# Layers: the index weights' rows scaled and signalled first, the values' up product behind a query product, the low part of y made right behind the row minima

## The chip, the cores and the metric

The kernel runs on one core of one Trainium2 chip. The metric is the device time of one execution in microseconds (us). Besides it stands the span: the time from the first to the last instruction in one profiled execution.

## The reference, cut to what matters

Two blocks follow each other on x (512 tokens, 1024 features). The first has two layers with three attention branches and a short convolution; it is the only part that the change touches.

```python
def first_block(x, ...):
    for l in range(DEPTH):                       # DEPTH = 2
        h = _rmsnorm(x, norm_g[l])
        p = _split(h @ w_in[l])
        o_a = _mla(p["a_cq"], p["a_ckv"], p["a_krope"], ...)
        o_b = _diff_attn(p["b_q"], p["b_k"], p["b_v"], ...)
        o_c = _dsa(p["c_q"], p["c_k"], p["c_v"], p["c_qidx"], p["c_kidx"], p["c_widx"], rel_bias, topk)
        o_d = _short_conv(p["d_b"], p["d_c"], p["d_h"], conv_w[l])
        y = jnp.concatenate([o_a * silu(a_gate), o_b * silu(b_gate), o_c * silu(c_gate), o_d * silu(d_gate)], -1)
        x = x + y @ w_out[l]
    return _rmsnorm(x, final_g)

# in _mla: q = rmsnorm(cq) @ w_uq;  kv = rmsnorm(ckv) @ w_ukv  -> k_nope, v
# in _dsa: score = relu(qidx . kidx);  index = sum over heads of widx * score;  top_k(index)
```

The second block (feed-forward, a mixture of dilated and block attention, cross attention, feed-forward) follows and is left as it is.

## The kernel before, in words

All matrices are kept transposed: features on the 128 partitions, the 512 tokens along a row. A product of fp32 accuracy is made of three passes over rounded parts: high times high, high times low and low times high. The weights come through a ring of four slots; ScalarE (ACT) makes the high part `whi` of a slot (L1632, one pass over 128x1024), VectorE (DVE, L2068) or GpSimd (POOL, L732) the low part `wlo`. TensorE (PE) runs the products of one column block of `w_in` as a "job" of eight chunks, three matmuls each (`products`, L963), into one of two PSUM banks `proj`; DVE or ACT evicts the bank and signals `job_free`.

Every engine has its own hand-written order; they meet through semaphores. Three places of a layer matter here.

**The index weights.** The job KR gives in one bank the index keys, the eight index weights (rows 0 to 8) and the rope part of the keys. DVE evicts it with four multiplications: `kidxT`, then `wT` (the weights, L2124), then two of `krope`, the last of which frees the bank. Between the first and the second stands `low_idx(1)`, a subtraction over 128x512 that makes a low part of the index queries (L2177); behind the last, `low_idx(2)` does that for the index keys. PE turns `wT` to token rows with four small matmuls (`turn_w`, L1041) in the middle of the job CQ0, and waits before them until the bank of KR is free (`wait_out(pe, L, "KR")`). ACT copies the result to `widx`.

**The attention steps.** A layer has 34 steps s. In a step PE makes the scores of step s (L1187), the products with the values of step s-3 (L1237), turns the probabilities of step s-2 (L1213), and then runs the fillers of that step: jobs, chunks and small products in the order of the tuple FILLERS, distributed over the steps by `fill_plan`. DVE makes `row_scales(s-1)`, `row_mins(s)` (L2112), early evictions, a piece of the top-k search, and the other evictions of the step; ACT copies the turned probabilities (L1823), makes the exponentials (L1658), and then handles the names of `ENDED[s]` one after the other: for each its copy and then, by `prepare_after`, the `whi` of the slot that hangs on this name. Names among the fillers: UKn, UVn and UQn are the up products of the MLA keys, values and queries. UK and UV all use one bank, `opsum[1]`; each waits until ACT has copied the one before (`up_out`). In step 4 PE runs UK1 and UQ1, in step 5 UV0 (L1123) and UQ2 (L1104), in step 6 UV1 and UQ3. The `whi` of the slot of GT1 hangs on UQ2. PE takes the scores of step s when the minima of step s-1 are made (`min_ready`).

**The low parts of y.** y is split chunk by chunk for the output product: ACT makes `yhi` at step `Y_HIGH[c]`, DVE `ylo` (`low_y`, L2082) in the step after, as the last thing of that step. The steps of `low_y` are 25, 26, 28, 28, 34, 35, 36 and 37 for the chunks 0, 2, 1, 3, 4, 5, 6 and 7. The output product follows the last step; it takes the chunks in that order, half of OUT0, half of OUT1, and then the other halves.

Of the kernel before, what the change touches and what calls it, by code (L numbers as in the profile page):

```python
# [27 lines left out]
KC = D // P  # L28
# [46 lines left out]
TAKE = ("QI0", "QI1", "KR", "KI", "CQ0", "CQ1", "CKV", "BQ0", "BK0", "VT0", "BQ1", "BK1", "VT1", "UK", "UV", "UQ",  # L75
        "GT0", "GT1", "GT2", "GT3", "DB0", "VT2", "DB1", "VT3", "SQ0", "SK0", "SQ1", "SK1", "DC0", "DC1",
        "GT4", "GT5", "DH0", "DH1", "GT6", "GT7") + tuple(f"OUT{c}" for c in range(KC))
FILLERS = ("BQ1", "VN0", "BK1", "VT1", "UK0", "UQ0", "UK1", "UQ1", "UV0", "UQ2", "UV1", "UQ3", "GT0", "VN1", "GT1", "GT2", "GT3",
           "DB0", "VT2", "DB1", "VN2", "VT3", "SQ0", "SK0", "VN3", "SQ1", "SK1", "SS0", "DC0", "SR0", "DC1", "SR1",
           "GT4", "GT5", "DH0", "DH1", "GT6", "GT7")  # L80
JOBS = ("QI0", "QI1", "KR", "CQ0", "CQ1", "CKV", "BQ0", "BK0", "VT0") + tuple(n for n in FILLERS if n[:2] not in ("VN", "UK", "UV")) \
    + tuple(f"OUT{c}" for c in range(KC))
# [162 lines left out]
def fill_plan():  # L245

    pieces = []
    for name in FILLERS:
        if name in SLOT_OF:
# [18 lines left out]
END = {name: s for s, fills in enumerate(PLAN) for name, k in fills}  # L268
ENDED = [[name for name in FILLERS if END[name] == s] for s in range(FILL_STEPS)]

# [3 lines left out]
for _fills in PLAN:  # L274
# [12 lines left out]
Y_HIGH = {0: C_STEP, 1: O_STEP[3] + 1, 2: END["SR0"] + 1, 3: END["SR1"] + 1, 4: O_STEP[4] + 1, 5: O_STEP[5],  # L287
          6: max(END["GT6"], END["DH0"]) + 3, 7: max(END["GT7"], END["DH1"]) + 3}
Y_ORDER = sorted(range(KC), key=lambda c: (Y_HIGH[c], c))
# [77 lines left out]
def rounded(ap):  # L367

    return ap.bitcast(F32R)


def build(nc, x, wstream, params, gains, tab1, tab2, hot1, hot2, rope, ident_in, mem, lines1, lines2, out):
    ctx = ExitStack()
    with ctx:
        place = {}

        def sb(name, shape):
            t = ctx.enter_context(nc.sbuf_tensor(name, shape, F32))
            place[name] = nc.sbuf_base - 4 * int(np.prod(shape[1:]))
            assert int(np.prod(shape[1:])) < S // 2 or place[name] % 128 == 0  # L380
            return t

        def over(name, of, shape, word=0):

            return nc.alloc_sbuf_tensor_at(name, shape, F32, offset=place[of] + 4 * word)

        def sem(name):
            return ctx.enter_context(nc.semaphore(name))
# [18 lines left out]
        R = sb("R", [P, S])  # L407
# [39 lines left out]
        yhi = over("yhi", "arena", [P, KC, S], at[0])  # L447
# [21 lines left out]
        wT = pT[0:8, 1, :]  # L469
# [50 lines left out]
        idx_hi_ready, idx_lo_ready = sem("idx_hi_ready"), sem("idx_lo_ready")  # L520
        idx_done = sem("idx_done")
        kw_ready, kidx_out, kidx_moved = sem("kw_ready"), sem("kidx_out"), sem("kidx_moved")
        relu_ready, idx_added = sem("relu_ready"), sem("idx_added")
        topk_step = sem("topk_step")
        mask_ready, cbias_ready = sem("mask_ready"), sem("cbias_ready")
# [55 lines left out]
        def layer_job(L, name):  # L581

            return L * LAYER_JOBS + (PRE_JOBS + JOB[name])

        def bank_of(L, name):

            return layer_job(L, name) % 2

        def uses(L, name):

            return layer_job(L, name) // 2

        def wait_out(eng, L, *names):


            for b in range(2):
                last = max((JOB[name] for name in names if bank_of(L, name) == b), default=None)
                if last is not None:
                    eng.wait_ge(job_free[b], uses(L, JOBS[last]) + 1)
# [306 lines left out]
        def _(pe):  # L906
# [80 lines left out]
            for L in range(DEPTH):  # L987
# [48 lines left out]
                def turn_w(k):  # L1036

                    if k == 4:
                        wait_out(pe, L, "KR")
                        for t in range(NT):  # L1040
                            mm = pe.matmul(opsum[0][:, 8 * t:8 * (t + 1)], wT[:, t * P:(t + 1) * P], ident[0:8, 0:8],  # L1041
                                           start=True, stop=True)
                        mm.then_inc(wi_turned, 1)
# [36 lines left out]
                for n, name in enumerate(IDX_JOBS):  # L1080
                    for k in range(KC):
# [3 lines left out]
                        if (n, k) in LATENT_AT:  # L1085
                            c = LATENT_AT.index((n, k))
# [977 lines left out]
        def _(dve):  # L2064
# [14 lines left out]
            def low_y(count, c, high=yhi2):  # L2079

                dve.wait_ge(y_hi, count)
                dve.tensor_tensor(rounded(ylo[:, c, :]), yT[:, c, :], high[:, c, :], ALU.subtract).then_inc(y_ready, 1)  # L2082
# [37 lines left out]
            def scaled(dst, src, factors, scale=1.0):  # L2120

                if scale == 1.0:
                    return dve.tensor_tensor(dst, src, factors, ALU.mult)  # L2123
                return dve.scalar_tensor_tensor(dst, src, scale, factors, ALU.mult, ALU.mult)  # L2124
# [23 lines left out]
            for L in range(DEPTH):  # L2148
                def prepare_after(name):

                    for i in PREP.get(name, ()):
                        if not on_pool(i):
                            make_low(i % RING, half_of(i), L * LAYER_SPLIT + (split_no(i) + 1))

                def take(name):
                    dve.wait_ge(job_done, layer_job(L, name) + 1)
                    return proj[bank_of(L, name)]

                def out_of(name, dst, scale=1.0):

                    scaled(dst, take(name)[:, :], R[:, :], scale).then_inc(job_free[bank_of(L, name)], 1)
# [11 lines left out]
                def low_idx(n):  # L2173

                    src = qidxT[:, n, :] if n < 2 else kidxT
                    dve.wait_ge(idx_hi_ready, L * 3 + (n + 1))
                    dve.tensor_tensor(rounded(idx_lo[:, n, :]), src, idx_hi[:, n, :], ALU.subtract).then_inc(idx_lo_ready, 1)  # L2177
# [6 lines left out]

                src = take("KR")
                scaled(kidxT[32:64, :], src[32:64, :], R[32:64, :]).then_inc(kidx_out, 1)
                low_idx(1)
                scaled(wT, src[0:8, :], R[0:8, :], 1.0 / 16)
                scaled(krope[HD:HD + 32, 0, :], src[HD:HD + 32, :], R[HD:HD + 32, :])
                scaled(krope[HD + 32:P, 1, :], src[HD + 32:P, :], R[HD + 32:P, :]).then_inc(job_free[bank_of(L, "KR")], 1)  # L2190
                low_idx(2)

                b_scale = -(32 ** -0.5)
# [47 lines left out]
                def stage_v(n):  # L2241

                    if n >= 2:
                        dve.wait_ge(v_turned, L * 4 + (n - 1))
                    out_of(f"VT{n}", vstage[:, n % 2, :])

                for n, name in enumerate(B_NAMES[:2]):
                    src, hi, lo = B_PARTS[name]
# [114 lines left out]
                def evict(name):  # L2363

                    kind, n = name[:2], int(name[2])
                    if kind in ("GT", "BQ", "BK", "SQ", "SK", "DB", "DC"):
                        out_of(name, {"GT": yT[:, n, :], "BQ": bqT[:, n % 2, :], "BK": bkT[:, n % 2, :], "SQ": cqT[:, n % 2, :],
                                      "SK": ckT[:, n % 2, :], "DB": dB[:, n % 2, :], "DC": dC[:, n % 2, :]}[kind],
                               {"BQ": b_scale, "SQ": -(HD ** -0.5)}.get(kind, 1.0))
                    elif kind == "VT":  # L2370
                        stage_v(n)
                    elif kind == "DH":
                        conv(n, 0)
                    elif kind == "SS":
                        subln_mean()
                    elif kind == "SR":
                        subln_out(n)
                    prepare_after(name)
# [3 lines left out]
                for s in range(LAST_STEP + 1):  # L2382
                    if 1 <= s <= STEPS:
                        row_scales(s - 1)
                    if s < STEPS:
                        row_mins(s)
                    for name in EARLY[s] if s < FILL_STEPS else ():
                        evict(name)
                    if s < MASK_STEP:
                        for n in TOPK_AT[s]:  # L2390
                            topk_half(n)
                    if s == MASK_STEP:
                        mask()
                    if s in O_STEP:
                        o_out(O_STEP.index(s))
                    for name in ENDED[s - 2] if 2 <= s < FILL_STEPS + 2 else ():
                        if name[:2] == "GT":
                            gate(int(name[2]))
                    for name in ENDED[s - 1] if 1 <= s <= FILL_STEPS else ():
                        if name[:2] == "DH":  # L2400
                            conv(int(name[2]), 1)
                    for name in ENDED[s] if s < FILL_STEPS else ():
                        if name not in EARLY[s]:
                            evict(name)
                    for n, c in enumerate(Y_ORDER):
                        if Y_HIGH[c] + 1 == s:
                            low_y(L * KC + (n + 1), c, yhi)
                def next_gain():

                    dve.wait_ge(par_loaded, L * 16 + 32)  # L2410
# [416 lines left out]
```

## Time and profile before

| | us |
|---|---|
| median of three runs | 1811.5 |
| lowest, highest | 1811.14, 1812.63 |
| the profiled execution's own time | 1812.77 |
| its span | 1810.9 |

The profiled execution is 1.27 us above the median; 1.87 us of its time lie outside its span. PE is busy in 99% of the span, DVE in 58%, ACT in 41%, POOL in 22%. The two layers stand at about 25 to 330 us and 340 to 645 us; the second repeats the first 314.1 us later.

### The profile page before, as it was taken

How to read it: one execution, taken by the hardware profiler on the slowest of the kernel's cores; microseconds unless marked ns; L12 is line 12 of the kernel's file. 1: busy time of each engine (PE TensorE's matmuls, PEld its weight loads, DVE VectorE, ACT ScalarE, POOL GpSimd, SP SyncE). 2: the span in 40 equal slices, each digit the busy share in tenths (PEclk: the TensorE clock that was granted, in tenths of full speed). 3: DMA queues.
4: the chain of work that ended last, by engine and by line, in shares of the span. 5: the costliest groups of instructions: out<-in, count | busy, mean ns of one | idle time of the engine just before them, and what ended most of it. 6: DMA issues, size and time to landing. Idle time of an engine off the chain costs nothing.

```text
span 1810.9 us, 25324 instructions
## 1 busy us (share of the span) xinstructions
PE 1790.2 (99%) x9372; PEld 1447.0 (80%) x9372; DVE 1051.0 (58%) x2117; ACT 746.6 (41%) x1379; POOL 395.0 (22%) x235
## 2 busy tenths in 40 slices
PE   8999999999999999999999999999999999999998
PEld 5767778776777888888888878878888888888887
DVE  3879767587867764554433435555665655545333
ACT  5454554446455432322222355546444323323222
POOL 2345452444545220000000232130200200000000
PEclk9999999999999999999999999999999999999999
DMA  6222112322211242333333422223221333323332
GB/s 221 71 82 71 59 59 83 95 71 82 76 51 59 86 143 93 98 99 93 97 108 107 154 64 73 91 71 111 87 82 37 103 93 95 102 93 95 103 105 92
DMA packets 49621, 165.53 MB, mean 91 GB/s; under 512 B 5624, under 2 KB 6136, under 8 KB 49528
## 3 DMA queue, kind: packets, MB, share of 16 engines
q1 hardware_dynamic: 48232, 161.88, 28.7%
q10 hardware_dynamic: 1296, 2.42, 0.4%
q8 instruction: 57, 0.93, 0.2%
q14 instruction: 36, 0.29, 0.0%
HBM read 162.12 MB, written 2.17 MB: 91 GB/s over the span
## 4 chain that ended last, share of the span: by engine, by line
PE 93%; DVE 4%; issue 2%; ACT 1%; DMA 0%; POOL 0%; SPq 0%; DVEq 0%; ACTq 0%
PE proj L963 75%; PE o L1237 2%; PE turned L1213 2%; PE score L1187 1%; PE turned L1439 1%; PE score L1430 1%; PE proj L1360 1%; PE o L1465 1%; PE proj L1367 1%; PE score L1196 1%; PE turned L935 1%; PE o L1544 1%; DVE arena L2206 1%; PE turned L947 1%; PE score L1533 1%
## 5 line engine op out<-in xcount | busy, mean ns | idle before, releaser
L963 PE MATMUL proj<-hhi,whi 128*128 128x512 f32 x1464 | 584.9, 400 | 0.6 <-DVE tanh L2123 0.3
L963 PE MATMUL proj<-hhi,wlo 128*128 128x512 f32 x1464 | 571.7, 390 | 0.0
L963 PE MATMUL proj<-hlo,whi 128*128 128x512 f32 x1464 | 570.9, 390 | 0.0
L1632 ACT ACTIVATE whi<-ring 128x1024 fp32r<-128x1024 f32 x280 | 296.2, 1058 | 638.6 <-PE proj L963 632.9
L2068 DVE TENSOR_TENSOR wlo<-ring,whi 128x1024 fp32r<-128x1024 f32 x200 | 244.3, 1221 | 168.2 <-ACT whi L1632 167.6
L963 PEld LDWEIGHTS proj<-hhi,whi 128*128 128x128 f32 x1464 | 275.8, 188 | 59.5 <-issue 6.6
L963 PEld LDWEIGHTS proj<-hhi,wlo 128*128 128x128 f32 x1464 | 275.2, 188 | 58.8
L963 PEld LDWEIGHTS proj<-hlo,whi 128*128 128x128 f32 x1464 | 275.8, 188 | 52.9
L732 POOL TENSOR_TENSOR wlo<-ring,whi 128x1024 fp32r<-128x1024 f32 x80 | 193.5, 2420 | 406.3 <-ACT whi L1632 405.7
L744 POOL TENSOR_TENSOR prob<-prob 128x512 f32<-128x512 f32 x36 | 56.9, 1579 | 877.2 <-ACT prob L1628 877.2
L1658 ACT ACTIVATE prob<-prob,negmax 128x256 f32<-128x256 f32 (+3 forms) x208 | 114.3, 552 | 60.8 <-DVE negmax L2112 59.7
L963 PE MATMUL proj<-inner_hi,wlo 128*128 128x512 f32 x352 | 136.9, 389 | 0.0
L963 PE MATMUL proj<-inner_hi,whi 128*128 128x512 f32 x352 | 136.9, 389 | 0.0
L963 PE MATMUL proj<-inner_lo,whi 128*128 128x512 f32 x352 | 136.9, 389 | 0.0
L2112 DVE CUSTOM_DVE_ANT_0 prob<-score,arena 128x256 f32<-128x256 f32 (+3 forms) x208 | 92.6, 482 | 60.5 <-PE turned L1439 55.3
L2123 DVE TENSOR_TENSOR tmp<-proj,R 128x512 f32<-128x512 f32 x48 | 33.2, 691 | 123.9 <-PE proj L963 117.8
L963 PE MATMUL proj<-yhi,whi 128*128 128x512 f32 x256 | 101.2, 395 | 0.6 <-DVE wlo L2068 0.5
L963 PE MATMUL proj<-yhi,wlo 128*128 128x512 f32 x256 | 99.9, 390 | 0.0
L963 PE MATMUL proj<-ylo,whi 128*128 128x512 f32 x256 | 99.5, 389 | 0.0
L2455 DVE TENSOR_TENSOR tmp<-tmp,proj 128x512 f32<-128x512 f32 x44 | 30.3, 688 | 103.8 <-PE proj L963 103.6
L1823 ACT ACTIVATE pT<-turned 128x128 f32<-128x128 f32 (+3 forms) x96 | 38.3, 433 | 104.7 <-PE turned L1213 104.1
L963 PEld LDWEIGHTS proj<-inner_hi,whi 128*128 128x128 f32 x352 | 66.1, 188 | 13.8
(304 smaller groups left out, 2394.3 us busy)
## 6 DMA issues: line engine op xcount, KB each, us to landing
ring<-wstream SPq DMA_DIRECT2D x288, 512.0 KB, 3.5
arena<-lines SPq DMA_DIRECT2D x28, 256.0 KB, 5.7
arena<-x ACTq DMA_DIRECT2D x4, 512.0 KB, 6.3
out<-arena SPq DMA_DIRECT2D x8, 256.0 KB, 2.7
arena<-mem SPq DMA_DIRECT2D x1, 1024.0 KB, 9.0
par<-params ACTq DMA_DIRECT2D x3, 74.0 KB, 1.8
arena<-hot SPq DMA_DIRECT2D x2, 80.0 KB
arena<-rope SPq DMA_DIRECT2D x1, 128.0 KB, 7.1
```

Of the source, the lines that this page charges most:

```text
L732: return pool.tensor_tensor(rounded(wlo[:, s, :]), ring[:, s, :], whi[:, h, :], ALU.subtract)
L744: pool.tensor_tensor(sq[:, 3, :], sq[:, 0, :] if c == 1 else sq[:, 3, :], sq_last if c == KC - 1 else sq[:, c % 3, :], ALU.add).then_inc(s ...
L963: mm = pe.matmul(b, rounded(w), rounded(rhs(v, k)), start=(first and n == 0 and p == 0), stop=(last and n == len(blocks) - 1 and p == 2))
L1213: mm = pe.transpose(turned[g % 2][:, kb * P:(kb + 1) * P], prob[:, (2 * s + n) % 4, kb * P:(kb + 1) * P], ident[:, :])
L1237: mm = pe.matmul(opsum[o % 2][h * HD:(h + 1) * HD, qb * P:(qb + 1) * P], v, pT[:, (g - 1 + h) % 4, kb * P:(kb + 1) * P], start=(kb == 0), ...
L1632: act.activation(rounded(dst), src, ACT.Copy, scale=scale).then_inc(ready, 1)
L1658: act.activation(prob[:, i, 0:W], prob[:, i, 0:W], ACT.Exp, bias=negmax[:, i:i + 1], scale=-1.0, accum_out=rowsum[:, i:i + 1] if total is ...
L1823: act.activation(pT[:, g % 4, 0:W], turned[g % 2][:, 0:W], ACT.Copy).then_inc(turn_out, 1)
L2068: dve.tensor_tensor(rounded(wlo[:, s, :]), ring[:, s, :], whi[:, h, :], ALU.subtract).then_inc(lo_ready, 1)
L2112: dve.tensor_tensor_reduce(prob[:, i, 0:W], src[:, 0:W], bias, 1.0, 3e38, ALU.add, ALU.min, negmax[:, i:i + 1]).then_inc(min_ready, 1)
L2123: return dve.tensor_tensor(dst, src, factors, ALU.mult)
L2455: dve.tensor_tensor(tmp[:, s, :], tmp[:, s, :], proj[(j + 1) % 2][:, :], ALU.mult)\
```

## The change

It has three parts.

1. The eviction of the index weights `wT` is moved ahead of `low_idx(1)` and gets a semaphore of its own, `wt_ready`; PE waits for that before `turn_w`, no longer for the bank. `low_idx(1)` moves behind the two evictions of `krope`.
2. In FILLERS, UV0 and UQ2 change places. The plan stays as it was but for the order in step 5; ACT's copies follow that order.
3. `low_y` moves from the end of a step to the place behind the early evictions, ahead of the top-k, the evictions of attention outputs (`o_out`), the gates, the convolution and the other evictions.

```diff
-"UV0", "UQ2", "UV1", "UQ3"
+"UQ2", "UV0", "UV1", "UQ3"
...
+        wt_ready = sem("wt_ready")
...
                     if k == 4:
-                        wait_out(pe, L, "KR")
+                        pe.wait_ge(wt_ready, L + 1)
...
                 scaled(kidxT[32:64, :], src[32:64, :], R[32:64, :]).then_inc(kidx_out, 1)
-                low_idx(1)
-                scaled(wT, src[0:8, :], R[0:8, :], 1.0 / 16)
+                scaled(wT, src[0:8, :], R[0:8, :], 1.0 / 16).then_inc(wt_ready, 1)
                 scaled(krope[HD:HD + 32, 0, :], src[HD:HD + 32, :], R[HD:HD + 32, :])
                 scaled(krope[HD + 32:P, 1, :], src[HD + 32:P, :], R[HD + 32:P, :]).then_inc(job_free[bank_of(L, "KR")], 1)
+                low_idx(1)
                 low_idx(2)
...
                     for name in EARLY[s] if s < FILL_STEPS else ():
                         evict(name)
+                    for n, c in enumerate(Y_ORDER):
+                        if Y_HIGH[c] + 1 == s:
+                            low_y(L * KC + (n + 1), c, yhi)
...
                     for name in ENDED[s] if s < FILL_STEPS else ():
                         if name not in EARLY[s]:
                             evict(name)
-                    for n, c in enumerate(Y_ORDER):
-                        if Y_HIGH[c] + 1 == s:
-                            low_y(L * KC + (n + 1), c, yhi)
```

On ACT, steps 5 and 6 of layer 0, before (`arena<-o1` 128x512 are the copies of UV0 and UV1, `arena<-proj` those of UQ2, `whi` the high part of GT1's slot):

```order
L1658 ACTIVATE prob,rowsum<-prob,negmax 128x256
L1784 ACTIVATE arena<-o1 128x512
L1772 ACTIVATE arena<-proj0 96x512
L1773 ACTIVATE arena<-proj0 32x512
L1632 ACTIVATE whi<-ring 128x1024
L1823 ACTIVATE pT<-turned0 128x256
```

and after:

```order
L1659 ACTIVATE prob,rowsum<-prob,negmax 128x256
L1773 ACTIVATE arena<-proj0 96x512
L1774 ACTIVATE arena<-proj0 32x512
L1633 ACTIVATE whi<-ring 128x1024
L1785 ACTIVATE arena<-o1 128x512
L1824 ACTIVATE pT<-turned0 128x256
```

The copy of UV0 has moved behind both copies of UQ2 and behind the high part.

On DVE, step 26 and the start of step 27 of layer 0, before (`ylo` is `low_y` of chunk 2, `yT<-o,yT` is `o_out`, the three rows ahead of `ylo` evict DC1 and the sub-norm product SR1):

```order
L2316 TENSOR_TENSOR yT<-o,yT 128x512
L2123 TENSOR_TENSOR arena<-proj,R 128x512
L2357 SCALAR_TENSOR_TENSOR arena<-arena,proj 128x512
L2361 TENSOR_TENSOR yT<-arena,yT 128x512
L2082 TENSOR_TENSOR ylo<-yT,yhi 128x512
L2299 RECIPROCAL rrow<-rowsum 128x2
L2302 TENSOR_SCALAR prob<-prob,rrow 128x256 x2
```

and after:

```order
L2083 TENSOR_TENSOR ylo<-yT,yhi 128x512
L2317 TENSOR_TENSOR yT<-o,yT 128x512
L2124 TENSOR_TENSOR arena<-proj,R 128x512
L2358 SCALAR_TENSOR_TENSOR arena<-arena,proj 128x512
L2362 TENSOR_TENSOR yT<-arena,yT 128x512
L2300 RECIPROCAL rrow<-rowsum 128x2
L2303 TENSOR_SCALAR prob<-prob,rrow 128x256 x2
```

The subtraction has moved ahead of the two evictions that wait for PE.

## Rows read from the trace of the kernel before

**Rows 1.** The page: busy us (share of the span) and instructions.

```profile
PE 1790.2 (99%) x9372; PEld 1447.0 (80%) x9372; DVE 1051.0 (58%) x2117; ACT 746.6 (41%) x1379; POOL 395.0 (22%) x235
```

**Rows 2.** PE's waits: engine, line, whom for; us in total, times, longest.

```profile
PE score L1187 <- DVE negmax L2112: 2.5, 6, 0.7
PE o L1041 <- DVE arena L2123: 1.8, 2, 0.9
...
PE o L1123 <- ACT arena L1779: 1.5, 2, 0.7
```

**Rows 3.** Timeline of PE at the turn of the weights: start, duration, [idle before <-releaser].

```profile
41.05 1.05 PE L1041 MATMUL o<-ident,pT 8*128 8x8 f32 x8 [0.91 <-DVE arena L2123]
...
356.73 1.05 PE L1041 MATMUL o<-ident,pT 8*128 8x8 f32 x8 [0.91 <-DVE arena L2123]
```

**Rows 4.** Windows: us, busy PE, PEld, DVE, ACT, POOL, granted clock (PEclk), DMA.

```profile
40.00:45.00 5.00, 4.09 (x19) 3.32 (x19) 1.68 (x3) 2.00 (x4) 3.63 (x3) 0.85 0.31 126
45.00:50.00 5.00, 5.00 (x27) 3.59 (x26) 2.15 (x2) 3.01 (x6) 2.35 (x1) 0.81 0.35 105
...
355.00:360.00 5.00, 4.09 (x22) 3.23 (x21) 2.34 (x4) 2.66 (x5) 4.11 (x3) 1.00 0.45 170
```

**Rows 5.** Timeline of DVE in the eviction of KR, layer 1.

```profile
353.86 0.69 DVE L2177 TENSOR_TENSOR idx_lo<-arena,idx_hi 128x512 fp32r<-128x512 f32 x1
354.58 0.68 DVE L2124 SCALAR_TENSOR_TENSOR pT<-proj,R 8x512 f32<-8x512 f32 x1
355.28 1.40 DVE L2123 TENSOR_TENSOR arena<-proj,R 32x512 f32<-32x512 f32 x2
```

**Rows 6.** Timeline of PE in steps 5 and 6, layer 0: UV0, turn, UV1.

```profile
114.47 1.10 PE L1123 MATMUL o<-ring,arena 128*128 128x256 f32 x4 [0.73 <-ACT arena L1779]
...
118.96 0.44 PE L1213 MATMUL turned<-ident,prob 128*128 128x128 f32 x2
119.24 1.03 PE L1123 MATMUL o<-ring,arena 128*128 128x256 f32 x4
```

**Rows 7.** Timeline of ACT in steps 4 to 6, layer 0.

```profile
113.73 0.59 ACT L1779 ACTIVATE arena<-o 64x512 f32<-64x512 f32 x1
...
117.99 0.58 ACT L1784 ACTIVATE arena<-o 128x512 f32<-128x512 f32 x1
118.47 0.58 ACT L1772 ACTIVATE arena<-proj 96x512 f32<-96x512 f32 x1
119.06 0.59 ACT L1773 ACTIVATE arena<-proj 32x512 f32<-32x512 f32 x1
119.67 1.06 ACT L1632 ACTIVATE whi<-ring 128x1024 fp32r<-128x1024 f32 x1
120.75 0.38 ACT L1823 ACTIVATE pT<-turned 128x256 f32<-128x256 f32 x1
```

**Rows 8.** Timeline of DVE in steps 26 and 27, layer 0.

```profile
242.64 0.75 DVE L2357 SCALAR_TENSOR_TENSOR arena<-arena,proj 128x512 f32<-128x512 f32 x1 [0.82 <-PE proj L947]
...
245.15 1.78 DVE L2082 TENSOR_TENSOR ylo<-yT,yhi 128x512 fp32r<-128x512 f32 x1
246.85 0.15 DVE L2299 RECIPROCAL rrow<-rowsum 128x2 f32<-128x2 f32 x1
247.04 1.46 DVE L2302 TENSOR_SCALAR prob<-prob,rrow 128x256 f32<-128x256 f32 x2
248.42 0.55 DVE L2112 CUSTOM_DVE_ANT_0 prob<-score,arena 128x384 f32<-128x384 f32 x1
```

**Rows 9.** Timeline of POOL in steps 26 and 27, layer 0.

```profile
242.32 2.36 POOL L732 TENSOR_TENSOR wlo<-ring,whi 128x1024 fp32r<-128x1024 f32 x1 [3.60 <-ACT whi L1632]
244.64 3.44 POOL L829 TENSOR_TENSOR arena<-arena 128x512 f32<-128x512 f32 x2
```

**Rows 10.** Timeline of PE: the scores of step 28, layer 0.

```profile
249.51 0.33 PE L1187 MATMUL score<-ck_hi,cq_hi 64*128 64x128 f32 x2 [0.69 <-DVE negmax L2112]
```

**Rows 11.** Timeline of DVE: the last low parts of y, layer 0.

```profile
295.75 1.89 DVE L2082 TENSOR_TENSOR ylo<-yT,yhi 128x512 fp32r<-128x512 f32 x3
```

**Rows 12.** Timeline of PE: the last chunk of y in OUT0, layer 0.

```profile
297.99 0.39 PE L963 MATMUL proj<-yhi,whi 128*128 128x512 f32 x1
```

More of the change, by code:

```diff
@@ L77 @@
         "GT4", "GT5", "DH0", "DH1", "GT6", "GT7") + tuple(f"OUT{c}" for c in range(KC))
-FILLERS = ("BQ1", "VN0", "BK1", "VT1", "UK0", "UQ0", "UK1", "UQ1", "UV0", "UQ2", "UV1", "UQ3", "GT0", "VN1", "GT1", "GT2", "GT3",
+FILLERS = ("BQ1", "VN0", "BK1", "VT1", "UK0", "UQ0", "UK1", "UQ1", "UQ2", "UV0", "UV1", "UQ3", "GT0", "VN1", "GT1", "GT2", "GT3",
            "DB0", "VT2", "DB1", "VN2", "VT3", "SQ0", "SK0", "VN3", "SQ1", "SK1", "SS0", "DC0", "SR0", "DC1", "SR1",
```

## The prediction, made before the changed kernel ran

> **What bounds the kernel now.** I read the page first: TensorE is busy in 99% of the span [rows 1], so the kernel is bound by PE's own stream, and an edit that adds no matmul and takes none away can only give back what PE stands still, or add to it. That makes PE's waits the view to read next [rows 2]: in both layers together PE waits 1.8 us at L1041 for DVE, 1.5 us at L1123 for ACT, and 2.5 us at L1187 for the minima. Each part of the change aims at one of these lines. The reader should see how small they are: 5.8 us in all, 0.3% of the time. About 0.2% (3.6 us) is what a measurement of this kernel can tell from no change, so the question is whether the three gains come whole and whether one of them sets up a new wait. After that I read the timelines of the engine that waits and of the one that releases it at each place, and the granted clock around them. The layers repeat each other, so I work in one and count two.
>
> **Part 1, the weights' rows.** PE reaches the turn at 41.05 - 0.91 = 40.14 us in layer 0 and at 355.82 in layer 1 [rows 3]. The wait ends with the last `krope` row of DVE: 355.28 + 1.40 = 356.68 [rows 5]. After the change the weights' rows come second: they take the place of the subtraction, 353.86 to 354.5, over a microsecond ahead of PE. The wait goes whole: 2 x 0.91 = 1.82 us gained. What is queued behind: the two `krope` rows end 0.7 us earlier; the subtraction moves behind them and ends at about 356.7, still ahead of the second subtraction, which ACT's high part lets start at 356.9 in any case. The first matmul that needs both is a whole job's first chunk later. I cost this reordering at nothing; its cover is those 4 us of job. After it DVE and ACT follow PE (they wait for its results in each job), so the 0.91 us are not taken back.
>
> **The clock behind part 1.** In layer 0 the granted clock falls between the two levels, from 2.4 to 1.2 GHz, shortly after this wait: 0.85 over one stretch of 5 us and 0.81 over the next [rows 4]. That costs 5 x 0.15 + 5 x 0.19 = 1.70 us. What PE did before was to wait 0.91 us and then run eight matmuls of 8x8 for 1.05 us. Behind the same wait in layer 1 the clock stays at 1.00 [rows 4]. So this wait is at the edge of what lowers the clock, and without the wait I expect no fall: 1.70 us less than in the profiled execution. The median of the runs is 1.27 us below that execution; most of them seem to have run without the fall, so against the median this gives little or nothing.
>
> **Part 2, UV0 behind UQ2.** Here PE waits 0.73 us before UV0 [rows 6], for ACT's copy of UK1 at 113.73 to 114.32 [rows 7]; the wake-up takes 114.47 - 114.32 = 0.15. UQ2 needs none of it and fills the gap. So PE gains 0.73 us at this point and reaches the end of step 6's turn at about 118.5. But the tuple also orders ACT. Before, UV0's copy starts at 117.99, ends at 118.57, and UV1, which may only overwrite the bank after it, starts at 119.24 without waiting. After, ACT first makes the two copies of UQ2 and the high part that hangs on UQ2: in the trace these three run from 118.47 to 120.75, 2.28 us [rows 7]. ACT can't begin them earlier than 117.99, since the exponentials of step 5 stand ahead. UV0's copy then runs 117.99 + 2.28 = 120.27 to 120.85, and UV1 starts at 120.85 + 0.15 = 121.00 where it started at 119.24: 1.76 us later than before, with the 0.73 us swallowed. PE stands still for about 2.5 us. Queued behind are UQ3, the scores of step 7 and all that follows; none of it can run ahead, and the later waits of PE are for DVE, which itself waits for PE's turns in steps 7 to 10, so the delay passes through. Cost: 2 x 1.76 = 3.52 us. Bounds: a gain of 2 x 0.73 = 1.46 if the copy came in time after all, a loss of 3.52 by the rows; I take the loss, since the order of ACT is written out and each of its durations has a row.
>
> **The clock behind part 2.** A standstill of 2.5 us in one piece is longer than the 0.91 us after which the clock fell in layer 0 [rows 3, 4]. Bounds: no fall, or one fall in each layer at 1.70 us. One wait in two brought a fall before; I take one fall in two again, 1.70 us. The Trainium skill (TensorE: Matmul & The Clock Gate, HAM oscillation) ties the return to the low level to long waits for a DMA in which the array stands quite still; by that rule neither wait would lower the clock, and the time would be that of the first rival below. The trace speaks against it at L1041.
>
> **Part 3, the low part of y.** In step 26 DVE waits 0.82 us for PE before SR1's eviction [rows 8], and then the subtraction takes 1.78 us, where the same form takes 0.69 [rows 5], because POOL has three operations running on end [rows 9]. Behind it stand the row scales and minima of step 27, for which PE waits 0.69 us at 249.51 [rows 10]. Moved ahead of `o_out`, the subtraction runs at about 240.0, when POOL is idle, takes 0.69 us and delays the eviction of DC1 by 0.1 us; SR1's eviction still waits for PE at 242.64. The row scales start at 245.15 where they started at 246.85. But two scalings follow beside POOL's two operations of 1.72 us each (244.64 to 248.08). Upper bound of the gain: the wait goes whole, 0.69. Lower bound: the second scaling is held until POOL ends at 248.08 and ends 0.15 later, at 248.23; with the overlap of 0.08 seen before the minima start at 248.15 where they started at 248.42, 0.27. Between these I take the middle, 0.48: 2 x 0.48 = 0.96 us gained. The Trainium skill (SBUF — State Buffer, Who interferes with whom) says that VectorE and GpSimd hold a shared port pair in turn for a whole instruction and the loser is blocked; the long subtraction in rows 8 agrees, and by that rule the gain is nearer the lower bound, a total 0.4 us higher.
>
> The other place where this part changes an order is the end of a layer: two subtractions move ahead of `o_out` and of the last gate. The last one ends at 295.75 + 1.89 = 297.64 before [rows 11], and PE needs it at 297.99 [rows 12]. After, the last gate ends 0.6 later and the last high part and subtraction follow it, which gives about 297.85. It still fits, with 0.1 us to spare: nothing, and at most 0.1 per layer. At steps 25 and 28 nothing stands between the old and the new place.
>
> **The sum**, against the profiled execution's 1812.77: -1.82 + 3.52 - 0.96 = +0.74 for the waits, -1.70 for the fall that goes, +1.70 for one that comes: 1813.5 us, 0.11% above the median.
>
> **The rivals.**
> - *The new wait is there, the clock stays up.* 1812.77 + 0.74 - 1.70 = 1811.8. For it: layer 1 before, where the clock stayed up [rows 4]. Against it: the standstill is nearly three times as long.
> - *The clock falls in both layers.* 1811.8 + 2 x 1.70 = 1815.2, at the edge of what can be told from no change.
> - *Faster: no new wait* (the change does on ACT what it does on PE). -1.82 - 1.46 - 0.96 - 1.70 = -5.94: 1806.8. It needs UV0's copy done by 118.4, while ACT is still in the exponentials. I see nothing for it but an error in my reading of the order.
> - *Slower: the low clock lasts.* The place is the stretch behind UV1. If the granted clock stays at 1.2 GHz for a second stretch in one of the layers, because the products there are short and broken by the scores, it costs a third time 1.70: 1816.9. It decides from (1815.1 - 1811.8) / 1.70, about two stretches, on. For it: PE's work behind UV1 has more small matmuls than that behind L1041. Against it: in layer 0 before, one stretch sufficed [rows 4].
>
> **How the numbers follow.** Chances: one fall (1813.5) 0.36, no fall (1811.8) 0.26, both (1815.2) 0.20, no new wait (1806.8) 0.07, low clock lasting (1816.9 and more) 0.11. Half of the case of two falls counts as slower. Faster by over 0.2%: 0.07. Slower by over 0.2%: 0.10 + 0.11 = 0.21. Within 0.2%: 0.72. The range: below, no fall, part 3 at its upper bound (0.42 less), and the new wait shorter by some 0.5 us in each layer, about the length of one of the copies ahead of it (0.58 [rows 7]), 1810.4; above, two falls with part 3 at its lower bound, 1815.6.
>
> **What would show it.** In the profile after: no wait at the turn of the weights in either layer; the values' product UV1 waiting about 2.5 us, twice, for ACT's copy of UV0, which stands behind the high part; no wait, or one of up to 0.4 us, at the scores of step 28; a `ylo` of 0.7 us instead of 1.78; granted clock 1.00 at 40 to 50 and perhaps below 1 at 120 to 127 and 434 to 441. It would be wrong if UV1 starts at once, or if the wait at L1187 only moves to a later step.

## The result, and the profile after

| | before | changed |
|---|---|---|
| median of 12 runs, us | 1812.01 | 1814.95 |
| lowest, highest | 1809.77, 1814.39 | 1810.12, 1818.36 |
| ratio | | 1.0015, 95% interval 1.0008 to 1.0022 |
| profiled execution, its span | 1812.77, 1810.9 | 1810.12, 1808.3 |

The change makes the kernel slower by 0.15%, 2.9 us. The first thing to note is that the profiled execution of the changed kernel happens to be its fastest run, 4.8 us below its median. Read alone, the two profiles would say the opposite of the twelve runs. What sets the runs of the changed kernel apart is TensorE's granted clock, averaged over a run: it goes from 0.999 (1810.12 and 1810.85 us) over 0.998 (1812.80 to 1813.63), 0.997 (1814.14), 0.996 (1815.77 to 1816.31) and 0.995 (1817.19) to 0.994 (1817.86 and 1818.36). The profiled one is at 0.999. In its windows the clock stays up behind both new waits, and falls only in the last microseconds of the program (columns as in [rows 4]):

```profile
115.00:120.00 5.00, 3.04 (x12) 1.73 (x14) 4.04 (x13) 3.90 (x10) 3.65 (x3) 1.00 0.00 0
120.00:125.00 5.00, 5.00 (x27) 4.00 (x26) 4.34 (x17) 2.70 (x7) 2.83 (x2) 1.00 0.64 213
...
435.00:440.00 5.00, 5.00 (x25) 3.86 (x25) 4.49 (x18) 1.99 (x6) 2.11 (x2) 1.00 0.65 210
...
1795.00:1800.00 5.00, 4.65 (x32) 4.20 (x31) 1.34 (x3) 0.63 (x1) 1.01 (x1) 0.86 0.00 0
```

Nor is all of the difference between the two profiles the work of the change. PE starts with small matmuls that turn x, ahead of every edit. Before:

```profile
10.52 1.06 PE L924 MATMUL proj<-ident,arena 128*128 128x128 f32 x2
...
15.65 0.63 PE L924 MATMUL o<-ident,arena 128*128 128x128 f32 x2
...
18.66 0.47 PE L978 MATMUL proj<-hhi,whi 128*128 128x512 f32 x1 [1.51 <-DVE xT L2128]
```

and changed:

```profile
10.30 1.06 PE L925 MATMUL proj<-ident,arena 128*128 128x128 f32 x2
...
13.60 0.38 PE L925 MATMUL o<-ident,arena 128*128 128x128 f32 x2
...
17.23 0.47 PE L979 MATMUL proj<-hhi,whi 128*128 128x512 f32 x1 [1.51 <-DVE xT L2129]
```

The same pair of matmuls still takes 0.63 us at 15.65 us before, and only 0.38 us from 13.60 us on in the changed kernel, so the first product comes after 6.93 us instead of 8.14. These 1.2 us are in the profile of the changed kernel and no part of the change makes them. Why the fast matmuls begin sooner stays open: the same stretch takes 6.93 to 7.38 us in the six profiles of this case whose kernels have parts 1 and 3 together, and 7.81 to 8.24 in the four others.

PE's waits in the changed kernel (the columns are those of [rows 2]; lines are one further down than before):

```profile
PE o L1124 <- ACT arena L1785: 4.8, 2, 2.4
PE proj L979 <- DVE xT L2129: 1.5, 1, 1.5
PE score L1188 <- DVE negmax L2113: 0.8, 2, 0.4
```

Against [rows 2]: the line of the weights' turn is gone (it had 1.8 us), the scores wait 0.8 us instead of 2.5, and the values' up products wait 4.8 us instead of 1.5. The sum over these three lines is 5.6 us where it was 5.8. By this view, what parts 1 and 3 give back, part 2 takes.

The new wait on PE's timeline of the changed kernel, layer 0, steps 5 to 7 (start, duration):

```profile
109.52 1.88 PE L1105 MATMUL proj<-arena,ring 128*128 128x512 f32 x4
111.24 1.03 PE L1124 MATMUL o<-ring,arena 128*128 128x256 f32 x4
...
114.14 0.44 PE L1214 MATMUL turned<-ident,prob 128*128 128x128 f32 x2
116.96 1.10 PE L1124 MATMUL o<-ring,arena 128*128 128x256 f32 x4 [2.39 <-ACT arena L1785]
117.90 1.88 PE L1105 MATMUL proj<-arena,ring 128*128 128x512 f32 x4
```

and ACT beside it:

```profile
113.94 0.57 ACT L1773 ACTIVATE arena<-proj 96x512 f32<-96x512 f32 x1
114.53 0.59 ACT L1774 ACTIVATE arena<-proj 32x512 f32<-32x512 f32 x1
115.14 1.06 ACT L1633 ACTIVATE whi<-ring 128x1024 fp32r<-128x1024 f32 x1
116.22 0.60 ACT L1785 ACTIVATE arena<-o 128x512 f32<-128x512 f32 x1
```

UQ2 runs at 109.52 with no gap and UV0 behind it is done at 112.27. ACT turns to step 5 at 113.94, makes the two copies of UQ2 and the high part, and comes to UV0's copy only at 116.22. It ends at 116.82, and 0.14 us later UV1 starts. From 113.94 to 116.22 are 2.28 us, the same sum of three durations that the prediction took from [rows 7].

Part 3 on DVE's timeline of the changed kernel, steps 26 and 27 of layer 0:

```profile
237.81 0.68 DVE L2083 TENSOR_TENSOR ylo<-yT,yhi 128x512 fp32r<-128x512 f32 x1
238.41 0.67 DVE L2317 TENSOR_TENSOR yT<-o,yT 128x512 f32<-128x512 f32 x1
...
240.44 0.75 DVE L2358 SCALAR_TENSOR_TENSOR arena<-arena,proj 128x512 f32<-128x512 f32 x1 [0.75 <-PE proj L948]
...
242.95 0.15 DVE L2300 RECIPROCAL rrow<-rowsum 128x2 f32<-128x2 f32 x1
243.14 2.49 DVE L2303 TENSOR_SCALAR prob<-prob,rrow 128x256 f32<-128x256 f32 x2
245.56 0.55 DVE L2113 CUSTOM_DVE_ANT_0 prob<-score,arena 128x384 f32<-128x384 f32 x1
```

with POOL beside it:

```profile
242.44 3.04 POOL L830 TENSOR_TENSOR arena<-arena 128x512 f32<-128x512 f32 x2
```

and the scores of step 28 on PE, now without a bracket behind them:

```profile
246.65 0.33 PE L1188 MATMUL score<-ck_hi,cq_hi 64*128 64x128 f32 x2
```

The subtraction takes 0.68 us instead of 1.78 [rows 8], because POOL stands still where it now is. The row scales come sooner, but the two scalings are held beside POOL's pair and take 2.49 us instead of 1.46. From SR1's eviction to the minima it was 248.42 - 242.64 = 5.78 us [rows 8], now it is 245.56 - 240.44 = 5.12. These 0.66 us are just enough: PE comes when the minima are ready.

### The profile page after: what moved, and what is told of

It reads as the page before. It is cut to its first block, busy times and chain, and to the rows that moved or that the text cites. A ratio compares the mean times of both kernels' runs of the same rounds, so it can differ in the third digit from the quotient of the medians.

```text
span 1808.3 us, 25324 instructions
## 1 busy us (share of the span) xinstructions
PE 1787.4 (99%) x9372; PEld 1444.7 (80%) x9372; DVE 1054.1 (58%) x2117; ACT 747.0 (41%) x1379; POOL 394.3 (22%) x235
## 4 chain that ended last, share of the span: by engine, by line
PE 93%; DVE 3%; ACT 1%; issue 1%; DMA 0%; POOL 0%; SPq 0%; DVEq 0%; ACTq 0%
PE proj L964 76%; PE o L1238 2%; PE turned L1214 2%; PE score L1188 1%; PE turned L1440 1%; PE score L1431 1%; PE proj L1361 1%; PE o L1466 1%; PE proj L1368 1%; PE score L1197 1%; PE turned L936 1%; PE o L1545 1%; DVE arena L2207 1%; PE turned L948 1%; PE score L1534 1%
```

## The experiments

Two questions were open after the result. Which part costs what, and where do the 4.8 us between the changed kernel's fastest run and its median come from? Theory W: PE's new wait costs its own length, and the granted clock falls behind it, how often depends on how long PE stands still. Rival F: the falls of the clock have another source, and the wait costs its length alone. All runs below are beside runs of the kernel before on the same chip (medians 1812.04 us over 24 runs in the first set of four, 1811.82 over 30 in the second).

**Parts 1 and 3 without part 2.** FILLERS as before, the rest as changed:

```diff
-"UQ2", "UV0", "UV1", "UQ3"
+"UV0", "UQ2", "UV1", "UQ3"
```

> Parts 1 and 3 of the change without part 2 (UV0 stays ahead of UQ2). Theory W (the loss is the new wait of PE at UV1 and the falls of the clock behind it): both waits go, 2 x 0.91 + 2 x 0.69 = 3.2 us below the median of before (1812.0), so 1808.8, no wait over 1 us inside the layers, and a narrow spread since nothing is left that stands still over 1 us. Rival F (the clock falls have another source, such as the denser stream of matmuls; the wait alone costs 3.5 us): about 3.2 us lower for the waits but about 3 us of falls remain, 1810 to 1812, with a spread like that of the changed kernel (8 us).

Measured: 1808.0 us (1806.55 to 1810.9, 11 runs), ratio 0.9979 (0.9970 to 0.9988), mean clocks 0.997 to 1.000. That is 4.0 us below before, where the waits make 3.2, and 7.6 us below the changed kernel of the same set. So part 2 makes the change a loss, and rival F, which forecast 1810 to 1812 us, falls. The spread of 4.4 us is not one of the clock alone: a run of 1808.0 us has a mean clock of 1.000, and the fastest, 1806.55 us, has 0.998.

**ACT's copy of UV0 first.** The changed kernel with ACT's order in a step set apart from PE's:

```diff
                     if s < FILL_STEPS:
-                        for name in ENDED[s]:
+                        for name in sorted(ENDED[s], key=lambda name: name[:2] != "UV"):
```

> The changed kernel, but ACT handles UV0 ahead of UQ2 in step 5 (its copy of UV0, then the two copies of UQ2 and the high part), while PE keeps UQ2 ahead of UV0. Theory W: the copy of UV0 ends at about 114.5 on the changed kernel's time line, PE is at UV1 at about 114.5, so both the old wait of 0.73 and the new one of 2.4 are gone: 1808.8 - 1.5 = 1807.3 us, no fall of the clock behind it. Rival F: waits go but falls stay, 1809 to 1811. Rival B (the order on PE itself costs, not ACT's): still near 1815.

Measured: 1806.35 us (1805.6 to 1807.12, 6 runs), ratio 0.9969 (0.9957 to 0.9981). PE's waits in this kernel:

```profile
PE proj L979 <- DVE xT L2129: 1.5, 1, 1.5
PE score L1188 <- DVE negmax L2113: 0.8, 2, 0.4
PE turned L1440 <- DVE prob L2561: 0.6, 1, 0.6
```

Neither the old nor the new wait at the values' product is left. UQ2 still runs ahead of UV0 on PE, so the loss comes from ACT's order and not from PE's, and rival B falls. This is the fastest version of the case.

**Part 2 alone.**

```diff
-"UV0", "UQ2", "UV1", "UQ3"
+"UQ2", "UV0", "UV1", "UQ3"
```

> Part 2 alone: UQ2 ahead of UV0 in the tuple, parts 1 and 3 undone. Theory W: before plus 2 x 1.76 = 3.5 us for the wait plus one to two falls of the clock more: 1817 (1815.5 to 1819), PE's wait at UV1 2.4 us in each layer. Rival F: the clock falls don't depend on this wait: 1815.5.

Measured: 1819.27 us (1815.07 to 1819.77, 7 runs), ratio 1.0031 (1.0020 to 1.0042), mean clocks 0.996 to 0.998. PE's waits:

```profile
PE o L1123 <- ACT arena L1784: 4.8, 2, 2.4
PE score L1187 <- DVE negmax L2112: 2.2, 4, 0.7
PE o L1041 <- DVE arena L2123: 1.8, 2, 0.9
```

The wait grows by 3.3 us against [rows 2], the time by 7.2. The rest is in the windows of the profiled execution, which is the slowest of the seven, 1819.77 us:

```profile
40.00:45.00 5.00, 4.09 (x19) 3.40 (x19) 1.58 (x3) 1.91 (x4) 3.54 (x3) 0.84 0.30 120
45.00:50.00 5.00, 5.00 (x26) 3.58 (x26) 2.23 (x2) 3.09 (x6) 2.40 (x1) 0.82 0.29 105
...
120.00:125.00 5.00, 4.08 (x8) 1.85 (x8) 3.38 (x9) 2.70 (x8) 4.69 (x3) 0.69 0.00 0
125.00:130.00 5.00, 5.00 (x25) 3.76 (x25) 3.28 (x15) 2.88 (x7) 1.74 (x2) 0.97 0.62 213
435.00:440.00 5.00, 2.61 (x21) 1.98 (x18) 3.43 (x13) 4.94 (x13) 2.46 (x2) 0.93 0.00 0
440.00:445.00 5.00, 5.00 (x17) 2.29 (x16) 2.46 (x7) 2.08 (x5) 4.24 (x4) 0.73 0.19 34
```

Three falls: one behind the turn of the weights, as in the profile of before, and one behind UV1 in each layer, 1.7 us each (5 x (0.31 + 0.03)). Behind UV1 this is the prediction's case of a fall in both layers, but of part 2 alone and in its slowest run: the fastest of the seven, 1815.07 us, has a mean clock of 0.998, where this one has 0.996.

**The changed kernel once more.**

> The changed kernel once more, for the granted clock of each run beside the others: 1815 us (1810 to 1818), mean clock 0.994 to 0.999. Theory W: each 0.001 of mean clock is about 1.8 us, and the runs with the lowest clock are the slowest; without falls 1810. Rival F: time and clock go the same way in every kernel of this call, not in those with the wait alone.

Measured: 1815.65 us (1811.89 to 1818.91, 11 runs), ratio 1.0018 (1.0009 to 1.0027), mean clocks 0.994 to 0.999. This time the profiled execution is one with a low clock, 1817.92 us at 0.994, with the same three waits as in the first profile. Its windows:

```profile
115.00:120.00 5.00, 2.94 (x6) 2.09 (x7) 4.04 (x13) 3.93 (x9) 3.54 (x2) 0.61 0.00 0
120.00:125.00 5.00, 5.00 (x17) 2.50 (x17) 1.54 (x8) 1.98 (x4) 2.86 (x3) 0.71 0.27 65
220.00:225.00 5.00, 5.00 (x23) 3.68 (x23) 3.91 (x8) 1.60 (x4) 5.00 (x3) 0.69 0.28 94
225.00:230.00 5.00, 5.00 (x40) 3.92 (x39) 3.36 (x6) 4.30 (x14) 4.08 (x3) 0.97 0.00 0
435.00:440.00 5.00, 4.26 (x10) 1.75 (x10) 3.20 (x6) 2.55 (x7) 4.87 (x3) 0.69 0.00 0
440.00:445.00 5.00, 5.00 (x26) 4.08 (x26) 3.52 (x16) 2.88 (x7) 1.56 (x2) 0.97 0.63 210
535.00:540.00 5.00, 5.00 (x31) 3.67 (x30) 3.62 (x8) 1.77 (x4) 2.56 (x2) 0.93 0.38 107
540.00:545.00 5.00, 5.00 (x22) 4.13 (x21) 3.31 (x8) 3.49 (x10) 5.00 (x3) 0.73 0.00 0
```

Behind UV1 in layer 0 the clock is low for twice as long: 5 x (0.39 + 0.29) = 3.4 us. Behind UV1 in layer 1 it costs 1.7 us. And there are two falls in another place, 1.7 us each: between 220 and 230 and between 535 and 545 us, right behind the sub-norm's sum, which in layer 0 is this row of PE in that execution:

```profile
218.55 1.84 PE L936 MATMUL proj<-halves,arena 128*128 128x2 f32 x16
```

PE doesn't wait there, but for 1.8 us it runs matmuls of two columns. By these windows 8.5 us are lost to the clock. The spans of the two profiles of the changed kernel, 1816.0 and 1808.3 us, differ by 7.7, so the windows overstate the price a little: in layer 1, from the row of L936 over 128x1 ahead of the attention steps to the sub-norm's sum, PE takes 153.20 us here (382.85 to 536.05), with one fall behind UV1, and 151.58 in the first profile (378.32 to 529.90), without one: 1.6 us a fall.

**Half the wait.** The changed kernel, but the high part that hangs on UQ2 is made behind UV0's copy:

```diff
                                 copy_up_v(int(name[2]))
-                            prepare_after(name)
+                            if name == "UQ2":
+                                continue
+                            prepare_after("UQ2" if name == "UV0" else name)
```

> The changed kernel, but in step 5 ACT makes the copy of UV0 right behind the two copies of UQ2 and ahead of the high part of the next slot. The copy of UV0 ends 1.08 us earlier, so PE's wait at UV1 is 2.39 - 1.08 = 1.3 us instead of 2.39. Theory W (length of the standstill costs directly and also by falls of the clock): 2.2 us less for the waits and about 2 us less for falls, 1815.3 - 4 = 1811.3 us, spread 3 us, mean clock 0.997 or more. Rival F (falls as often behind 1.3 us as behind 2.4): 1813.1 us with mean clocks down to 0.994.

Measured: 1809.39 us (1808.13 to 1810.36, 11 runs), ratio 0.9987 (0.9978 to 0.9996), mean clocks 0.997 to 0.999. PE's wait:

```profile
PE o L1124 <- ACT arena L1785: 2.6, 2, 1.3
```

The wait is 4.8 - 2.6 = 2.2 us shorter and the time 1815.65 - 1809.39 = 6.3 us (the two were taken in different sets, beside the same kernel before within 0.2 us). So 4.1 us went that no wait accounts for; they went with the low clocks. The profile of this kernel is its fastest run, with no fall in the layers, so it doesn't show where the other runs fall. Against the version without this wait, 1806.66 in the same set, it is 2.7 us slower, for 2.6 us of wait: at 1.3 us a piece the wait costs its own length. At 2.4 us a piece it costs nearly double: the changed kernel is 1815.65 - 1806.35 = 9.3 us above that version, for 4.8 us of wait. This is what tells W from F, which expected as many falls behind 1.3 us as behind 2.4: more is lost to the clock behind the longer standstill, and more than theory W said, which put 2 us on it.

**Part 1 alone.**

```diff
                 scaled(kidxT[32:64, :], src[32:64, :], R[32:64, :]).then_inc(kidx_out, 1)
-                low_idx(1)
-                scaled(wT, src[0:8, :], R[0:8, :], 1.0 / 16)
+                scaled(wT, src[0:8, :], R[0:8, :], 1.0 / 16).then_inc(wt_ready, 1)
...
+                low_idx(1)
                 low_idx(2)
```

> Part 1 alone: the weights' rows first, with their own semaphore. Theory W: PE's wait of 0.91 us at the turn of the weights goes in both layers, and with it the falls of the clock behind it, which some runs of before have: 1812.0 - 1.8 - 0.5 to 1.0 = 1809.4 us. Rival G (DVE is late again a little later and the gain is given back at the latents' spread or at the first scores): 1811 to 1812, with the missing 0.9 us as a new wait before 85 us in layer 0.

Measured: 1808.8 us (1807.52 to 1811.5, 11 runs), ratio 0.9984 (0.9975 to 0.9993). It gains 3.0 us for 1.8 us of waits. No wait took their place: rival G falls. The rest, 1.2 us, fits the falls behind this wait that go too, as the mean clocks say (0.998 or less in 23 of 30 runs of before, 0.999 here in nine of eleven). But the profiled execution, one of the other two, has a fall of the second kind, behind the sub-norm's sum of layer 1, in a kernel that has no wait over 0.73 us in its layers:

```profile
530.00:535.00 5.00, 5.00 (x21) 3.72 (x20) 4.14 (x8) 1.99 (x5) 5.00 (x3) 0.66 0.18 70
```

**Part 3 alone.**

```diff
                     for name in EARLY[s] if s < FILL_STEPS else ():
                         evict(name)
+                    for n, c in enumerate(Y_ORDER):
+                        if Y_HIGH[c] + 1 == s:
+                            low_y(L * KC + (n + 1), c, yhi)
```

> Part 3 alone: low parts of y behind the minima. Theory W: PE's wait of 0.69 us at the scores of step 28 goes in both layers, the subtraction of chunk 2 takes 0.7 us instead of 1.78, nothing at the end of a layer: 1812.0 - 1.3 = 1810.7 us. Rival L (the two scalings behind it are held beside GpSimd's operations, and the delay only changes its owner): the scalings take 2 to 2.5 us, the wait stays at about 0.4, 1811.4 us.

Measured: 1810.45 us (1809.45 to 1812.74, 11 runs), ratio 0.9995 (0.9986 to 1.0004). The waits of PE on the minima and, beside them, DVE's scalings:

```profile
PE score L1187 <- DVE negmax L2112: 1.1, 4, 0.4
```

```profile
244.87 2.49 DVE L2302 TENSOR_SCALAR prob<-prob,rrow 128x256 f32<-128x256 f32 x2
```

The waits fall from 2.5 to 1.1 us, 1.4 us, and the median from 1811.82 by 1.4. The interval includes no change, so the time alone doesn't show it; the profile does. Rival L was right about the scalings and wrong about the wait. This profile too has a fall behind the sub-norm's sum of layer 1:

```profile
530.00:535.00 5.00, 5.00 (x32) 3.73 (x31) 3.62 (x7) 1.58 (x2) 2.81 (x2) 0.91 0.32 107
535.00:540.00 5.00, 5.00 (x25) 4.05 (x23) 3.39 (x8) 3.74 (x11) 5.00 (x4) 0.74 0.00 0
```

**The fastest version once more.**

> The version with ACT's copy of UV0 first once more, beside its parts: 1806.4 us again (1805.5 to 1807.5), ratio to before 0.9969, mean clock 0.998 or more in every run. If the gains of parts 1 and 3 and of the mended part 2 add up: 1812.0 less part 1's and part 3's measured gains less 1.5 for the wait of 0.73 at UV0, twice.

Measured: 1806.66 us (1805.59 to 1808.25, 8 runs), ratio 0.9973 (0.9963 to 0.9984). The parts nearly add up: 3.0 of part 1, 1.4 of part 3 and the 1.5 that the expectation put on the mended part 2 are 5.9 us, and 1811.82 - 1806.66 is 5.2. The trace says which of them is too large. Between the same two rows of L936 PE takes, in layer 0, 149.68 us in the profile of parts 1 and 3 (64.41 to 214.09) and 149.21 in the first one of this version (64.17 to 213.38), and in layer 1 again 0.5 us less. Filling the gap of 0.73 us gives back 0.5 and not 0.73; 3.0, 1.4 and 1.0 are 5.4.

This version has the second kind of fall as well. In this profile (1807.9 us, the second slowest of the eight), where PE's longest wait in the layers is 0.4 us:

```profile
525.00:530.00 5.00, 5.00 (x31) 3.66 (x30) 3.62 (x8) 1.76 (x4) 2.56 (x2) 0.92 0.34 107
530.00:535.00 5.00, 5.00 (x22) 4.12 (x22) 3.26 (x8) 3.49 (x10) 5.00 (x3) 0.74 0.00 0
```

## Why the prediction was right, and where a term was off

- *The time.* 1814.95 us lies in the range of 1810.4 to 1815.6, 1.4 us above the forecast. It is slower than before by a measured 0.15%, within the 0.2% that the forecast's main case stayed in. The waits were worked out rightly; that the clock's share brought the total so near was in part luck, as the last points show.
- *Part 1.* Right: the wait is gone in both layers, 1.8 us, and nothing took its place. The reordering behind it costs nothing: the two subtractions run end to end (353.10 to 354.98 us in layer 1) and no wait follows.
- *The clock behind part 1.* The fall behind this wait goes, as forecast, and at about the forecast price: part 1 alone gives 1.2 us more than its waits. But the prediction read the runs of before wrongly. It said that most of them had run without this fall, so that its going would give little or nothing against the median. 23 of 30 have mean clocks of 0.998 or less, and all three profiles with this wait (before, part 2 alone, part 3 alone) have the fall in layer 0 and none in layer 1.
- *Part 2, the wait.* Right in mechanism, and in size: UV1's wait was forecast at 2.5 us and is 2.39. It follows from reading ACT's order, not PE's. Of the 3.52 us of the sum, the waits view shows 4.8 - 1.5 = 3.3. The path shows a little more: between the same two rows (L935 before, L936 now) PE takes 151.53 us in layer 0 (64.07 to 215.60) where it took 149.68 before (68.13 to 217.81), and in layer 1 151.58 where it took 149.68 (382.22 to 531.90), together 3.75 more.
- *Part 3.* Under-sized. The term was 0.48 us a layer; the whole 0.69 came. The scalings were held as feared (2.49 us), but POOL's pair ended sooner than in the profile of before (3.04 us against 3.44 [rows 9]), since the subtraction no longer stood between its two operations. The lower bound had its mechanism right, the second scaling ends 0.15 us behind POOL's pair (245.63 and 245.48), but had taken POOL's old end as fixed. The prediction's remark that by the port rule the gain would be nearer the lower bound went wrong for the same reason; it came at the upper one. At the end of a layer nothing was lost, as forecast.
- *The clock.* This term was mis-sized. One fall in two like waits was taken over from [rows 3] and [rows 4] to a standstill 2.6 times as long. The median of the changed kernel is 4.8 us above its run without a fall in the layers, about three stretches of 1.6 to 1.7 us, not one. The slower rival (the low clock lasting behind UV1) does occur: layer 0 in the second profile of the changed kernel. What the prediction missed altogether is the second place, behind the two-column matmuls.
- *The size of both terms together.* The waits of the three lines come to -0.2 us, where the sum had +0.74; along PE's path it is about +0.5 (1.8 and 1.4 gained, 3.75 lost). The clock behind the new waits was put at +1.70 us, and the median run lost some 4.8 against the run without a fall. That run, 1810.12 us, is itself 1.7 us below the 1811.8 that the prediction gave to this case; 1.2 of that is the stretch ahead of the first product, which the sum did not have. The errors have opposite signs, so the total missed by 1.4 us and not by more: that is luck, and no sign that the clock term was understood.

What stays open: why the clock falls behind the two-column matmuls in some runs and not in others. They are no effect of part 2 or of a long wait: the profiles of part 1 alone, of part 3 alone and of the fastest version have one such fall each, the second profile of the changed kernel has two, and the other six have none with the same rows. That a fall behind UV1 shifts the later work to where the next one strikes was only argued, and it can't be the whole reason, since three of those four profiles have no fall behind UV1. So the falls follow the length of the wait only in part, and which share of the 4.8 us lies behind UV1 in the median run no trace shows; in the one run with a low clock that was profiled it was three stretches of five.

## What to carry to other kernels

A table that sets one engine's order often sets another's as well. Before an instruction is moved to fill a gap, read the order on the engine that evicts its result: here 1.5 us of gap on TensorE were traded for 4.8 us behind ScalarE, and one line that keeps ScalarE's order apart turned a loss of 0.15% to 0.18% into a gain of 0.3%. In a kernel bound by TensorE, a wait's price here had two parts, its length and the clock behind it. Where the mean granted clock differs between runs, one profile may show the best of them, and two profiles can differ by more than the change before they reach its first edit: here by 1.2 us of 2.7.

## What the runs showed of the hardware that was not expected

- From 1.3 to 2.4 us a piece, what the clock cost grew faster than the wait. With 1.3 us of wait per layer, 11 runs had mean clocks of 0.997 to 0.999 and spread over 2.2 us; with 2.4 us, 23 runs of the changed kernel had 0.994 to 0.999 and spread over 8.8 us (1810.12 to 1818.91).
- Falls also come with no wait just before, behind 1.84 us of matmuls of two columns, while PE counts as busy: granted clock 0.69 at 220 to 225 us and 0.73 at 540 to 545 in the second profile of the changed kernel, 0.66, 0.74 and 0.74 in those of part 1 alone, part 3 alone and the fastest version.
- The Trainium skill (TensorE: Matmul & The Clock Gate, HAM oscillation) tells of falls behind long waits for a DMA. Here waits of 0.91 us for VectorE followed by narrow matmuls, and of 2.39 us for ScalarE, were enough, by the granted clock of 0.85 [rows 4] and of 0.61 behind them, though neither brings a fall each time.
- A subtraction on VectorE moved out from between two GpSimd operations shortened those too: 3.44 us [rows 9] became 3.04 for the pair, and 3.04 again in the profile of part 3 alone.
